# Up pass of an MLP in seven products: five take the high weights against both parts in 512 columns, and the first product is accumulated on in the fourth one's bank

## The reference, cut to what matters

```python
D_MODEL = 2048
SEQ = 512
D_FF = 4 * D_MODEL

def reference(x, norm_mix_g, w_in, ..., norm_mlp_g, w_mlp_up, w_mlp_down, norm_final_g):
    h = x
    ...                                   # mixing: recurrent branch, attention branch, gates
        h = h + mixed @ w_out[l]
        u = rms_norm(h, norm_mlp_g[l])
        h = h + jnp.square(jax.nn.relu(u @ w_mlp_up[l])) @ w_mlp_down[l]
    return rms_norm(h, norm_final_g)
```

## Time and profile before

| | before |
|---|---|
| median of 3 runs | 2521.72 us (2520.69 to 2523.28) |
| profiled execution, its own time | 2520.72 us |
| its span | 2518.9 us |
| TensorE busy | 2499.6 us (99%), 13123 matmuls |
| VectorE busy | 1960.1 us (78%) |
| ScalarE busy | 1279.5 us (51%) |
| GpSimd busy | 552.5 us (22%) |
| mean DMA rate | 183 GB/s |

### The profile page before, as it was taken

One profiled execution on the slowest core, in us unless ns is written; L12 is line 12 of the kernel. 1 busy time (PEld: TensorE's weight loads), 2 busy tenths in 40 slices (PEclk: granted clock), 3 DMA queues, 4 the chain that ended last, 5 costly groups with the idle time before them and its releaser, 6 DMA issues.

```text
span 2518.9 us, 35468 instructions
## 1 busy us (share of the span) xinstructions
PE 2499.6 (99%) x13123; PEld 2163.5 (86%) x13123; DVE 1960.1 (78%) x2060; ACT 1279.5 (51%) x1622; POOL 552.5 (22%) x452
## 2 busy tenths in 40 slices
PE   9999999999999999999999999999999999999998
PEld 8888888888888888888899999999998888888886
DVE  5878875556479978843588888888889999999997
ACT  6432384344354554423466666666665454544555
POOL 3650131002100000000011221111221453433434
PEclk9999999999999999999999999999999999999999
DMA  6472323223754764453356665566668695545652
GB/s 199 151 267 84 103 88 96 83 74 102 295 195 151 310 250 190 145 167 133 103 161 201 207 202 187 187 202 201 205 204 326 234 291 209 219 162 202 233 217 84
DMA packets 257152, 460.91 MB, mean 183 GB/s; under 512 B 10369, under 2 KB 150241, under 8 KB 243745
## 3 DMA queue, kind: packets, MB, share of 16 engines
q1 hardware_dynamic: 243920, 414.87, 47.6%
q0 software_dynamic: 12880, 44.57, 5.9%
q10 hardware_dynamic: 256, 0.18, 0.0%
HBM read 366.13 MB, written 93.32 MB: 182 GB/s over the span
## 4 chain that ended last, share of the span: by engine, by line
PE 84%; issue 10%; DVE 4%; DMA 1%; ACT 1%; POOL 0%; ACTq 0%; POOLq 0%; DVEq 0%
PE stream L2324 9%; PE stream L2325 9%; PE stream L2326 9%; PE stream L2745 4%; PE stream L2746 4%; PE stream L2747 4%; PE aux L2746 4%; PE aux L2747 4%; PE aux L2745 4%; PE aux L2713 4%; PE stream L2713 3%; PE aux L2724 2%; PE aux L2723 2%; PE aux L2722 2%; PE stream L2724 2%
## 5 line engine op out<-in xcount | busy, mean ns | idle before, releaser
L1579 DVE TENSOR_TENSOR wlo<-raw,whi 128x2048 fp32r<-128x2048 f32 x72 | 173.5, 2410 | 190.5 <-ACT whi L950 190.5
L911 POOL TENSOR_TENSOR hh<-hh,dn_tmp 128x512 f32<-128x512 f32 x112 | 219.0, 1975 | 328.7 <-ACT dn_tmp L1473 328.7
L950 ACT CAST whi<-raw 128x2048 fp32r<-128x2048 f32 x72 | 137.4, 1908 | 228.1 <-PE stream L2326 228.1
L1512 ACT CAST dhi<-d 128x1024 fp32r<-128x1024 f32 x160 | 167.7, 1053 | 162.6 <-PE aux L2747 96.6
L2324 PE MATMUL stream<-uhi,whi 128*128 128x512 f32 (+1 forms) x640 | 244.0, 381 | 2.5 <-DVE wlo L1579 2.5
L2325 PE MATMUL stream<-ulo,whi 128*128 128x512 f32 (+1 forms) x640 | 242.9, 380 | 0.0
L2326 PE MATMUL stream<-uhi,wlo 128*128 128x512 f32 (+1 forms) x640 | 242.8, 379 | 0.0
L2252 DVE TENSOR_TENSOR dlo<-d,dhi 128x1024 fp32r<-128x1024 f32 x160 | 228.3, 1445 | 11.5 <-ACT dhi L1512 11.4
L2745 PE MATMUL stream<-dhi,dsum 128*128 128x512 f32 x448 | 174.4, 389 | 1.2 <-DVE hh L2177 1.2
L2746 PE MATMUL stream<-dlo,dsum 128*128 128x512 f32 x448 | 174.3, 389 | 0.0
L2747 PE MATMUL stream<-dhi,dsum 128*128 128x512 f32 x448 | 174.3, 389 | 0.0
(11 more groups left out here) (405 smaller groups left out, 7310.7 us busy)
## 6 DMA issues: line engine op xcount, KB each, us to landing
d<-in_w_mlp_down SPq DMA_DIRECT2D x64, 1024.0 KB, 7.5
dsum<-sums_d SPq DMA_DIRECT2D x56, 1024.0 KB, 10.8
raw<-in_w_in SPq DMA_DIRECT2D x48, 1024.0 KB, 5.2
g<-in_w_in SPq DMA_DIRECT2D x32, 1024.0 KB, 7.1
up_b<-in_w_mlp_up SPq DMA_DIRECT2D x32, 1024.0 KB, 11.4
up_a<-in_w_mlp_up SPq DMA_DIRECT2D x32, 1024.0 KB, 9.8
gsum<-usum_d SPq DMA_DIRECT2D x28, 1024.0 KB, 9.5
sums_d<-hlo SPq DMA_DIRECT2D x32, 896.0 KB, 4.3
```

The source lines that it names most:

```text
L911: pool.tensor_tensor(v, v, dn_tmp[r][:], ALU.add).then_inc(s.dn_p, 1)
L950: nc.scalar.copy(whi[slot][:, 0:width], raw[slot][:, 0:width]).then_inc(s.hi_ready, 1)
L1512: nc.scalar.copy(dhi[m % 7][:], parts[j]).then_inc(s.half_hi, 1)
L1579: V.tensor_tensor(wlo[slot][:, 0:width], raw[slot][:, 0:width], whi[slot][:, 0:width].bitcast(F32), ALU.subtract).then_inc(s.lo_ready, 1)
```

## The change

Products 2, 4, 5, 6 and 1 are wide, products 0 and 3 narrow (before: 1, 3 and 5 wide). Bank A thus has a running sum in two halves, and the copies of it after products 2 and 4 take 512 columns. Product 0 is copied by ScalarE into the left half of bank B in place of SBUF, and product 3 is added on it there, without an opening matmul; its sum is the first output, whose ReLU ScalarE reads from the bank. One matmul ahead of the second pair writes bank B of the `aux` set once. `hid_out` becomes three instructions of 512 columns, all ahead of product 2's weights. Product 6's two halves are added by a reduction on VectorE (`hid_last`), ahead of product 4's weights, and ScalarE takes its ReLU in SBUF. The same moves are made where the last pair meets the down pass.

```diff
@@ the copies between SBUF places
+    states = at("states", 62, [P, 34 * HALF], F32)
+
+    def spaced(first, step):
+        return states[:, HALF * first:HALF * (first + 2 * step)].rearrange("p (c n) -> p c n", c=2)[:, :, 0:HALF]
+
+    snap_u2, snap_u3 = spaced(0, 1), spaced(9, 8)
+    left, right = spaced(0, 9), spaced(1, 16)
+    state_q = at("state_Q", 204.0 + 1.8125, [P, 2, HALF], F32)
+    def by_column(b):
+        return b[:].rearrange("p (c n) -> p n c", c=2)
@@ up_act (ScalarE)
                 if j == 1 and not first:
                     act.wait_ge(s.up_c, 3 * i)
-                    nc.scalar.copy(snap["U3"][:], a_old).then_inc(s.up_snap, 1)
-                if j == 3 and not first:
-                    nc.scalar.activation(c21[:], a_old, ACT.Relu).then_inc(s.up_snap, 1)
+                    nc.scalar.copy(snap_u3, a_old).then_inc(s.up_snap, 1)
                 if j == 4 and not first:
-                    act.wait_ge(s.up_c, 3 * i + 1)
-                    nc.scalar.copy(snap["P1"][:], a).then_inc(s.up_snap, 1)
+                    act.wait_ge(s.up_c, 3 * i)
+                    nc.scalar.copy(up_bank(u, 3)[:, 0:HALF], up_bank(u, 0)[:, 0:HALF]).then_inc(s.up_snap, 1)
...
                 if j == 6:
-                    act.wait_ge(s.up_c, 3 * i + 2)
-                    nc.scalar.copy(snap["U2"][:], a).then_inc(s.up_snap, 1)
+                    act.wait_ge(s.up_c, 3 * i + 3)
+                    nc.scalar.copy(snap_u2, a).then_inc(s.up_snap, 1)
@@ hid_relu (ScalarE)
             act.wait_ge(s.up_c, 3 * i + 6)
-            nc.scalar.activation(up_out[:, :, 0:HALF], up_out[:, :, 0:HALF], ACT.Relu).then_inc(s.up_relu, 1)
-            act.wait_ge(s.up_snap, 5 * i + 5)
+            nc.scalar.activation(up_out[:, 0, 0:HALF], up_bank(u - 1, 3)[:, 0:HALF], ACT.Relu).then_inc(s.up_relu, 1)
+            nc.scalar.activation(up_out[:, 1:3, 0:HALF], up_out[:, 1:3, 0:HALF], ACT.Relu).then_inc(s.up_relu, 1)
+            act.wait_ge(s.up_part, 3 * i + 3)
+            nc.scalar.activation(c21[:], c21[:], ACT.Relu).then_inc(s.up_relu, 1)
+            act.wait_ge(s.up_relu, 3 * i + 3)
@@ hid_out and hid_last (VectorE)
-                if j in (0, 2) and not first:
+                if j == 2 and not first:
                     hid_out(i - 1, u - 1, j)
+                if j == 4 and not first:
+                    hid_last(i - 1, u - 1)
...
+            dve.wait_ge(s.up_snap, 4 * i + 4)
+            V.tensor_tensor(snap_u2, halves(up_bank(u, 5)), snap_u2, ALU.subtract).then_inc(s.up_part, 1)
+            V.tensor_tensor(snap_u3, state_q[:], snap_u3, ALU.subtract).then_inc(s.up_part, 1)
+            dve.wait_ge(s.up_part, 3 * i + 2)
+            V.tensor_tensor(up_out[:, 1:3, 0:HALF], left, right,
+                            ALU.add).then_inc(s.up_c, 3)
+
+        def hid_last(i, u):
+            dve.wait_ge(s.up_mm, 7 * i + 4 + 7)
+            if not isinstance(i, int) or i:
+                dve.wait_ge(s.up_sq, 2 * i + 1)
+            V.tensor_reduce(c21[:], by_column(up_bank(u, 6)), AX.X, ALU.add).then_inc(s.up_part, 1)
@@ dn_dve (VectorE)
-                if first and m in (0, 2):
+                if first and m == 2:
                     hid_out(PAIRS - 1, 3, m)
+                if first and m == 3:
+                    hid_last(PAIRS - 1, 3)
@@ up_pe (TensorE)
-                    pe.wait_ge(s.up_snap, 5 * i + {2: 1, 4: 3, 5: 2, 6: 4}[j])
+                    pe.wait_ge(s.up_snap, 4 * i + {2: 1, 4: 3, 5: 2, 6: 4}[j])
...
-                opens = j in (0, 1, 3)
-                if AT[j] != "A":
+                opens = j in (0, 1)
+                if j in (0, 3):
                     for q in range(q0, q1):
...
+        up_pe(0, 0, True)
+        pe.wait_ge(s.up_lo, 7 + 1)
+        T.matmul(up_bank(1, 3)[:], uwhi[3][:, 0], both_parts(0, 0), start=True, stop=True)
+        for u in range(1, 4):
+            up_pe(u, u, False)
```

More of the change, by code:

```diff
@@ L1368, in up_act @@
             _, _, _, _, parts = up_parts(u)
-            a, c = up_bank(u, 0)[:, 0:HALF], halves(up_bank(u, 1))
-            a_old = up_bank(u + 1, 0)[:, 0:HALF]
+            a, c = halves(up_bank(u, 0)), halves(up_bank(u, 1))
+            a_old = halves(up_bank(u + 1, 0))
             for j in range(4 if first else 0, 7):
@@ L1417, in hid_square @@
             begun = not isinstance(i, int) or i >= 1
-            act.wait_ge(s.up_relu, i + 1)
+            act.wait_ge(s.up_relu, 3 * i + 3)
             if begun:
@@ L1446, in _ @@
         act.wait_ge(s.up_mm, 5)
-        act.wait_ge(s.up_c, 1)
-        nc.scalar.copy(snap["P1"][:], up_bank(0, 0)[:, 0:HALF]).then_inc(s.up_snap, 1)
+        nc.scalar.copy(up_bank(0, 3)[:, 0:HALF], up_bank(0, 0)[:, 0:HALF]).then_inc(s.up_snap, 1)
         sum_hi_parts(7, LATE, 24 + 8)
@@ L1485, in dn_act @@
                     act.wait_ge(s.up_c, 3 * PAIRS)
-                    nc.scalar.copy(snap["U3"][:], up_bank(3, 0)[:, 0:HALF]).then_inc(s.up_snap, 1)
-                if first and m == 3:
-                    nc.scalar.activation(c21[:], up_bank(3, 0)[:, 0:HALF], ACT.Relu).then_inc(s.up_snap, 1)
+                    nc.scalar.copy(snap_u3, halves(up_bank(3, 0))).then_inc(s.up_snap, 1)
                 if m == 2 and not (first or begins):
@@ L2092, in hid_out @@
             dve.wait_ge(s.up_mm, 7 * i + 8 + j)
-            dve.wait_ge(s.up_snap, 5 * i + {0: 1, 2: 4}[j])
-            if j == 0:
-                dve.wait_ge(s.up_sq, 2 * i + 2)
-                if isinstance(i, int) and i == 0:
-                    dve.wait_ge(s.ss2_ok, 16)
-            parts = [(up_bank(u, 3), 0, snap["P1"], ALU.add)] if j == 0 else \
-                [(up_bank(u, 5), 1, snap["U2"], ALU.subtract), (None, 2, snap["U3"], ALU.subtract)]
-            for b, x, part, op in parts:
-                left = b[:, 0:HALF] if b else state_q[:, 0]
-                V.tensor_tensor(up_out[:, x, 0:HALF], left, part[:], op).then_inc(s.up_part, 1)
-            for b, x, part, op in parts:
-                right, v = b[:, HALF:S] if b else state_q[:, 1], up_out[:, x, 0:HALF]
-                dve.wait_ge(s.up_part, 3 * i + x + 1)
-                V.tensor_tensor(v, v, right, ALU.add).then_inc(s.up_c, 1)
+            dve.wait_ge(s.up_sq, 2 * i + 2)
+            if isinstance(i, int) and i == 0:
+                dve.wait_ge(s.ss2_ok, 16)
+            dve.wait_ge(s.up_snap, 4 * i + 4)
[9 more added lines that the diff above has]
+            V.tensor_reduce(c21[:], by_column(up_bank(u, 6)), AX.X, ALU.add).then_inc(s.up_part, 1)
         def hid_lo(i):
@@ L2709, in both @@
                     return bk[:] if q in sums_near else halves(bk)
-                opens = j in (0, 1, 3)
-                if AT[j] != "A":
+                opens = j in (0, 1)
+                if j in (0, 3):
                     for q in range(q0, q1):
-                        T.matmul(both(q), uwhi[k][:, q], both_parts(q, j), start=opens and q == 0, stop=False,
-                                 skip_group_check=True)
-                    for q in range(q0, q1):
-                        ins = T.matmul(dst, uwlo[k][:, q], shi[q][:, j], start=False, stop=q == KP - 1,
-                                       skip_group_check=True)
@@ L2718, in up_pe @@
-                for q in range(q0, q1):
-                    wh, wl, sh, sl = uwhi[k][:, q], uwlo[k][:, q], shi[q][:, j], slo[q][:, j]
-                    if AT[j] != "A":
-                        continue
-                    T.matmul(dst, wh, sh, start=opens and q == 0, stop=False, skip_group_check=not opens)
-                    T.matmul(dst, wh, sl, start=False, stop=False, skip_group_check=not opens)
-                    ins = T.matmul(dst, wl, sh, start=False, stop=q == KP - 1, skip_group_check=not opens)
+                        wh, wl, sh, sl = uwhi[k][:, q], uwlo[k][:, q], shi[q][:, j], slo[q][:, j]
@@ new lines, in up_pe @@
+                        T.matmul(dst, wh, sh, start=opens and q == 0, stop=False, skip_group_check=True)
+                        T.matmul(dst, wh, sl, start=False, stop=False, skip_group_check=True)
+                        ins = T.matmul(dst, wl, sh, start=False, stop=q == KP - 1, skip_group_check=True)
+                    if q1 == KP:
+                        ins.then_inc(s.up_mm, 1)
+                    continue
+                for q in range(q0, q1):
+                    T.matmul(both(q), uwhi[k][:, q], both_parts(q, j), start=opens and q == 0, stop=False,
+                             skip_group_check=True)
@@ L2725, in up_pe @@
+                for q in range(q0, q1):
+                    ins = T.matmul(dst, uwlo[k][:, q], shi[q][:, j], start=False, stop=q == KP - 1,
+                                   skip_group_check=True)
                 if q1 == KP:
                     ins.then_inc(s.up_mm, 1)
-        for u in range(4):
-            up_pe(u, u, u == 0)
+        up_pe(0, 0, True)
[3 more added lines that the diff above has]
+            up_pe(u, u, False)
```

2 lines of the change are left out of this document (removed).

## The result

| | before | after |
|---|---|---|
| median, runs beside each other on one chip | 2521.97 us (2520.69 to 2523.28, 4 runs) | 2556.28 us (2556.13 to 2556.54, 4 runs) |
| span of the profiled execution | 2518.9 us | 2554.3 us |
| up pass ends at (first matmul of the down pass) | 1898.5 us | 1932.0 us |

The ratio is 1.0139, 95% interval 1.0127 to 1.0151. The forecast was 2516.8 us with a range up to 2520.0, so it was wrong by 39.5 us and in its sign. The spans differ by 35.4 us. Of these 33.5 lie in the up pass, which starts at 1258.3 and 1258.2; the other 1.9 lie behind it.

A forecast was written before the change was run, and what follows sets the result against it. The prediction took TensorE's stream, 19.90 us a pair, as the bound. Wider products -5.8, an added matmul +0.23 and the passes' meeting +0.65 gave -4.9 us: 2516.8 us from a median of 2521.72, range 2514.9 to 2520.0.

The forecast's parts named there:

- TensorE's stream: Up pass: two more of seven products a pair become wide, saving 5.8 us in all (4.7 to 6.3).
- W: Time of one wide product on TensorE, put at 2.78 us against 2.89 us for a narrow one.
- rival C: Up-pass products: columns set the pace, so wide and narrow cost the same; 2522.6 us, chance 0.08.
- the sum: All terms for the whole kernel together: -5.8 + 0.23 + 0.65 = -4.9 us, giving 2516.8 us.
- The copies: ScalarE's copies after products 2 and 4 grow from 0.38 to 0.57 us; product 0's goes to PSUM; all hidden.
- The meeting: Where up and down pass meet, VectorE's added work makes slot 6 late: 0.65 us more (0.4 to 1.2).
- T: Rival where the passes meet: a second late slot or late load adds some 2 us; 2519 us, chance 0.09.
- The reduction's own price: VectorE's reduction of product 6 from PSUM, taken as 0.6 us net, ends 0.4 and 1.2 us.
- D: Rival: VectorE's reduction from PSUM is slow, at 3.5 us holding up each pair; 2535 us, chance 0.08.
- "Hidden.": VectorE in a pair: 0.5 us more work fits its 3.04 us idle less 0.19, so costs nothing.
- the distance of 5 us: Product 5's low part is ready at 1509.44, TensorE wants it at about 1514.7, so order matters little.
- The wait for the reduction: ScalarE's wait ahead of product 6's ReLU: about nothing, the reduction ending near 1505.5 as earlier ReLUs finish.

The follow-up runs named there:

- e3: Changed kernel with ScalarE's `hhi` cast moved behind the next pair's cast for product 0; 2517.45 us, ratio 0.9983 to the kernel before.
- f1: Changed kernel without the reduction; ScalarE reads product 6's left half alone, leaving the right half out of one output; 2517.13 us, ratio 0.9982.
- b2: Kernel before with a fifth GpSimd instruction of 256 columns in each pair, into a spare place; 2572.54 us, ratio 1.0201.
- b3: Kernel before with a fifth GpSimd instruction a pair and the `hhi` cast behind the next pair's first weight cast; 2521.27 us, ratio 0.9999.
- e2: Changed kernel with the reduction one low part earlier, ahead of product 3's in place of product 4's; 2552.06 us, ratio 1.0119.
- e5: Changed kernel with the `hhi` cast behind the next pair's first weight cast and a fifth GpSimd instruction a pair; 2545.16 us, ratio 1.0093.

## Why the prediction was wrong

**TensorE's stream: right.** 5.8 us less was forecast (4.7 to 6.3). In e3 the up pass, from 1258.3 to 1893.3, is 5.2 us shorter, 5.4 without the added matmul, at 19.73 us a pair against 19.90. W is 2.79 us, also for a wide product behind a wide one (in e3 products 5 and 6 start at 1493.21 and 1496.00), so the mechanism of the rival C is out, though the period of 19.8 or more that was its sign came. e3 ends at 2517.45 and f1 at 2517.13, where the sum said 2516.8.

**The copies: right. The meeting: dearer than the sum had it.** A new wait of 0.4 to 1.2 us was forecast for a `dlo` at the start of the down pass; it is 0.6 in the changed kernel and 0.5 in e3. The later slots slip a little too: the down pass's ninth slot (its 97th matmul) starts 23.17 us behind the first in the changed kernel and 22.87 in e3, 21.79 before. So the meeting costs 1.4 us in the one, 1.1 in the other, where the sum had 0.65 and T's sign began at 1.5. Another 0.5 us in either trace lies further on in the down pass, which the sum had not looked at. The copy of product 0 to PSUM takes 0.36 us, bounds 0.3 and 0.6.

**The reduction's own price: right.** 0.6 net and 0.4 to 1.2 were said; it is 0.68, 0.60 from start to start. D forecast slower, and its sign in the trace, TensorE waiting for `uwlo` in each pair, is what came. Its mechanism did not: it needed a reduction of 3 us.

**The step that failed** is "Hidden." at the end of the paragraph on VectorE in a pair, with the sentence behind it on the distance of 5 us that "repeats in every pair", and the same for ScalarE and GpSimd ("GpSimd gets its squares 0.5 us later and is idle four fifths of the time"). I compared VectorE's added 0.5 us with the 3.04 us that VectorE is idle. Idle time is cover only for work whose results nobody needs at once. VectorE's idle times were waits for ScalarE's casts, and I never followed ScalarE further: `hhi` stands ahead of cast 0 in its order and waits for GpSimd, who waits for squares, which stand behind a cast that needs VectorE's sum and, with the change, behind the reduction too. The new edge made that turn the longest one, and the cover that counted was not 3.04 us but the difference between TensorE's pair and one turn: 1.2 to 1.3 us without the reduction (the estimate and the row at f1), which the wait for it and its ReLU more than used up. I also took GpSimd's instructions at what they cost in VectorE's idle time. The row that said otherwise was in the profile of before: 0.73, 0.74, 1.81, 0.74 us for four instructions of one form, the long one beside VectorE's low part.

**The wait for the reduction** was forecast to be about nothing, with the reduction ending near 1505.5 just as ScalarE's ReLUs were done. ScalarE waits 1.02 us for it. The forecast held VectorE's position in the pair fixed by TensorE, while VectorE's stretch slides with the loop.

What is shown: the place of one ScalarE wait decides over 38.8 us (e3), a GpSimd instruction costs 50.8 or nothing by that place (b2, b3), and the reduction, or ScalarE's wait for it, is needed for the loss (f1). What is only argued: the account of 0.2 us over the edge. What stays open: why the GpSimd instruction of 3.33 us in b2 had to let three of VectorE's pass, when in e2 it came in behind the first; no kernel here ran GpSimd beside VectorE instructions of other forms on purpose.

## What to carry to other kernels

An engine's idle time is slack only if what it waits for doesn't depend on its own earlier work. Before adding an edge between in-order engines, follow the waits backwards from a waiting instruction until they come back to the same engine one iteration earlier, count an instruction that merely stands behind a waiting one as waiting too, and compare the sum of that turn with the pace of the engine that should set the time.

A loss that comes from such a loop is taken back most cheaply by the order: e3 moves one cast behind another and is the best version that computes all of its outputs (2517.45 us, 0.17% under before), though by the estimate at e5 it has only 0.6 to 1.8 us to spare. And in pricing a turn, an engine that another one can hold up has two prices, so a small delay can cost more than itself.
